# Making the four q units of the sparse attention in the front instead of in the group loop

## The chip, the cores and the metric

The kernel runs on one core of a Trainium2 chip. A core has five engines that run side by side and meet only at semaphores: PE (TensorE, the matrix products; its weight loads are listed apart as PEld), DVE (VectorE), ACT (ScalarE), POOL (GpSimd) and SP (SyncE, which issues DMAs; ACT issues some too). The metric is the device time of one launch in microseconds: the median of several runs.

## The reference, cut to what matters

The program is one transformer block with three mixers, followed by a second block of two layers. The change touches only the first block's input projection and its sparse attention:

```
h = rmsnorm(x, g_pre_mix);  z = h @ w_in                      # x is 512 x 1024
q_nsa, kv_nsa, g_nsa, qkv_ml, if_ml, o_ml, q_mem, g_merge = split(z)
q = q_nsa.reshape(B, S, 4 groups, 4 heads, 64)                # the "q units": 256 columns a group
kc, vc = compress_blocks(k), compress_blocks(v)               # 31 compressed keys and values
o_cmp = masked_softmax(q . kc) @ vc                           # compressed branch
o_slc, o_win = selected and window branches: masked_softmax(q . k) @ v over 512 tokens
y_nsa = gb0 * o_cmp + gb1 * o_slc + gb2 * o_win
h_ml  = mlstm_chunkwise(...)  ->  y_ml = sigmoid(o_ml) * rmsnorm(h_ml) * ml_head_g
y_mem = memory_xattn(...)
gm = sigmoid(g_merge)                                         # three gates of 1024 columns
y = gm0 * (y_nsa @ W_nsa) + gm1 * (y_ml @ W_ml) + gm2 * (y_mem @ W_mem)
```

## The kernel before

**Weights as units.** All weights pass through the same path in units of 1024 x 256 numbers. SP loads a unit into one of two raw buffers; ACT copies it rounded into `w_hi` (L663 in loops, L671 else); POOL subtracts to get the rest, `w_lo` (L1090, L1096; DVE does it in the later feed-forward stages); PE multiplies. Each product is made of three matmuls (hi by hi, hi by lo, lo by hi: L1126 to L1128, or L1154 to L1156 where the result has tokens on the partitions), so one unit is 48 matmuls of 512 columns.

**The front.** The table `UNITS` lists 22 units and `SCHEDULE` writes out by hand in which order units and small steps stand on all engines. The tail of the front is the mLSTM mixer. For each of its four heads, `ml_scores(h)` makes one broadcast product and four score products on PE (L1314, L1319), between which DVE and ACT make the decay and the mask (L1814, L826, L1824, L1827); `ml_out(h)` multiplies by the values (L1330), and then DVE and ACT normalise (L1834 to L1837, L832, L834), which PE waits for before the next head. At the end `ml_norm` scales the result (L1852) and `ml_turn` transposes it on PE (L1340) and splits it on ACT and DVE (L849, L1858).

**The group loop.** The sparse attention runs four times round a loop (one group of four heads each). PE's order in a group: the 48 products of the q unit into banks 0 and 1; 18 matmuls of merge gates (`GATE_PRE`); a wait for `q_split`, while ACT (L875) and DVE (L1884, L1888) split q into the stacked form `q_st`; 16 pairs of compressed scores of 32 columns (L1391, L1392); then 35 steps, each with the scores of step i, the transposes of step i-2 (L1416), the weighting of step i-3 (L1426) and three gate matmuls (L1365); then the transposes of the compressed probabilities (L1442), 12 gate matmuls, the compressed outputs (L1449), the last gate matmuls, and the transposes of the result (L1456). The gate matmuls, 144 in a group, come from three further units and fill PE's time while ACT and DVE work on the softmax. DVE masks the scores (L1930), ACT takes the exponential (L881), both copy the transposed probabilities (L889, L1938). ACT also copies gate tiles out (L899) at the steps named in `GATE_EVAC` and makes `w_hi` of the coming units behind some of these copies. SP loads the eight pieces of the group's keys from DRAM once the group before is finished.

## Time and profile before

| | |
|---|---|
| runs | 3099.30, 3088.74, 3098.14 us; median 3098.14 |
| profiled execution | 3098.84 us, of which 3096.8 us from the first to the last instruction |
| PE busy | 2908.8 us, 94% of the span |
| DVE, ACT, POOL busy | 1467.1, 889.7, 327.5 us |
| mean granted clock of PE | 0.967 of 2.4 GHz |
| mLSTM tail of the front | 273.97 to 371.63 us |
| the four groups | begin at 371.63, 473.36, 573.87 and 672.81 us, merge begins at 774.62 us |

Engines work side by side, so busy times don't add up to the span. A timeline row gives start, length, engine, line, operation, output and inputs, shapes, count, and in brackets the idle time before it and what ended it. PE's single matmuls overlap: how fast they go is the distance of their starts, not their length.

### The profile page before, as it was taken

The page shows a single profiled execution, that of the slowest core. Times are in us where ns is not written, and L with a number is a line of the kernel's source. Part 1 is how long each engine was busy: PE and PEld are TensorE (multiplying, and loading weights), DVE is VectorE, ACT ScalarE, POOL GpSimd, SP SyncE. Part 2 cuts the span into 40 slices and gives each one's busy share as a digit, 9 for nine tenths or more (in the row PEclk, how much of TensorE's full clock was granted, in tenths as well). Part 3 has the DMA queues.
Part 4 walks back from the last instruction along what each step waited for, and adds up shares of the span by engine and source line. Part 5 has one row for each costly group of instructions (what it writes and reads, how often), then busy time and mean ns, then how long its engine had stood idle before and what let it go on. Part 6 is the DMA issues. An engine that isn't in the chain of part 4 may idle for free.

```text
span 3096.8 us, 34841 instructions
## 1 busy us (share of the span) xinstructions
PE 2908.8 (94%) x13510; PEld 2385.9 (77%) x13510; DVE 1467.1 (47%) x2140; ACT 889.7 (29%) x1214; POOL 327.5 (11%) x62
## 2 busy tenths in 40 slices
PE   6998799999998999899999899999999889899997
PEld 6777688888777888778888788887888765578886
DVE  2334344445457443365433644434543479454432
ACT  4333443334233222232222322222222231422221
POOL 4222111111310000000000000000000066100000
PEclk9998899999999999999999999999999999999999
DMA  6222112221441232322232232232223221222221
GB/s 190 87 65 69 55 42 82 72 72 48 142 156 55 95 105 91 102 68 95 95 114 66 81 97 96 98 104 79 95 95 99 78 68 41 68 68 95 96 98 72
DMA packets 255085, 270.54 MB, mean 87 GB/s; under 512 B 5695, under 2 KB 243407, under 8 KB 254858
## 3 DMA queue, kind: packets, MB, share of 16 engines
q1 hardware_dynamic: 250688, 261.87, 26.2%
q10 hardware_dynamic: 4298, 7.36, 0.7%
q8 instruction: 61, 1.00, 0.1%
q14 instruction: 38, 0.31, 0.0%
HBM read 258.72 MB, written 10.49 MB: 87 GB/s over the span
## 4 chain that ended last, share of the span: by engine, by line
PE 71%; issue 16%; POOL 5%; DVE 5%; ACT 2%; DMA 1%; SPq 0%; POOLq 0%; DVEq 0%; ACTq 0%
PE bank L1126 21%; PE bank L1127 20%; PE bank L1128 20%; POOL w_lo L1096 3%; POOL w_lo L1090 3%; PE bank L1620 1%; PE bank L1141 1%; PE bank L1142 1%; PE bank L1143 1%; DVE rstd L2052 1%; ACT w_hi L671 1%; PE bank L1154 1%; PE bank L1156 1%; PE bank L1155 1%; PE bank L1271 0%
## 5 line engine op out<-in xcount | busy, mean ns | idle before, releaser
L1126 PE MATMUL bank<-h_hi,w_hi 128*128 128x512 f32 x2064 | 816.2, 395 | 53.8 <-POOL w_lo L1096 25.4
L1127 PE MATMUL bank<-h_lo,w_hi 128*128 128x512 f32 x2064 | 810.8, 393 | 0.0
L1128 PE MATMUL bank<-h_hi,w_lo 128*128 128x512 f32 x2064 | 810.3, 393 | 0.0
L2008 DVE TENSOR_TENSOR w_lo<-w_raw,w_hi 128x2048 fp32r<-128x2048 f32 (+2 forms) x176 | 390.2, 2219 | 389.1 <-ACT w_hi L671 322.3
L1126 PEld LDWEIGHTS bank<-h_hi,w_hi 128*128 128x128 f32 x2064 | 392.3, 190 | 145.0 <-POOL w_lo L1096 29.6
L1127 PEld LDWEIGHTS bank<-h_lo,w_hi 128*128 128x128 f32 x2064 | 392.3, 190 | 82.6 <-issue 1.2
L1128 PEld LDWEIGHTS bank<-h_hi,w_lo 128*128 128x128 f32 x2064 | 392.0, 190 | 82.3
L1096 POOL TENSOR_TENSOR w_lo<-w_raw,w_hi 128x2048 fp32r<-128x2048 f32 x34 | 217.1, 6391 | 1930.2 <-ACT w_hi L671 1930.2
L1126 PE MATMUL bank<-hid_hi,w_hi 128*128 128x512 f32 x880 | 343.4, 390 | 0.0
L1128 PE MATMUL bank<-hid_hi,w_lo 128*128 128x512 f32 x880 | 342.4, 389 | 0.0
L1127 PE MATMUL bank<-hid_lo,w_hi 128*128 128x512 f32 x880 | 342.4, 389 | 0.0
L663 ACT ACTIVATE w_hi<-w_raw 128x2048 fp32r<-128x2048 f32 x124 | 236.9, 1911 | 355.3 <-PE bank L1128 347.9
L671 ACT ACTIVATE w_hi<-w_raw 128x2048 fp32r<-128x2048 f32 (+2 forms) x110 | 199.5, 1818 | 411.5 <-PE bank L1128 401.5
L964 ACT ACTIVATE gate_tmp<-gate_tmp 128x512 f32<-128x512 f32 x110 | 67.7, 632 | 483.8 <-DVE gate_tmp L2099 483.8
L2107 DVE TENSOR_TENSOR gate_tmp<-gate_tmp,bank 128x512 f32<-128x512 f32 x110 | 75.6, 687 | 252.7 <-PE bank L1128 250.7
L1126 PEld LDWEIGHTS bank<-hid_hi,w_hi 128*128 128x128 f32 x880 | 165.2, 188 | 34.6 <-issue 0.5
L1127 PEld LDWEIGHTS bank<-hid_lo,w_hi 128*128 128x128 f32 x880 | 165.2, 188 | 34.6 <-issue 0.5
L1128 PEld LDWEIGHTS bank<-hid_hi,w_lo 128*128 128x128 f32 x880 | 165.2, 188 | 34.3
L2099 DVE TENSOR_TENSOR gate_tmp<-bank,rstd 128x512 f32<-128x512 f32 x110 | 70.9, 686 | 182.7 <-PE bank L1128 182.5
L1090 POOL TENSOR_TENSOR w_lo<-w_raw,w_hi 128x2048 fp32r<-128x2048 f32 x24 | 110.2, 4594 | 435.3 <-ACT w_hi L663 435.3
L881 ACT ACTIVATE prob<-prob,nsa_stat 128x512 f32<-128x512 f32 (+3 forms) x128 | 71.8, 561 | 158.0 <-DVE nsa_stat L1930 157.9
L1930 DVE CUSTOM_DVE_ANT_0 prob<-bank,const_masks 128x512 f32<-128x512 f32 (+3 forms) x128 | 62.8, 491 | 113.6 <-PE bank L1392 72.5
(362 smaller groups left out, 3437.0 us busy)
## 6 DMA issues: line engine op xcount, KB each, us to landing
w_raw<-in_ffn_w_in_dram SPq DMA_DIRECT2D x88, 1024.0 KB, 5.0
w_raw<-in_w_in_dram SPq DMA_DIRECT2D x32, 1024.0 KB, 5.3
w_raw<-in_ffn_w_out_dram SPq DMA_DIRECT2D x32, 1024.0 KB, 5.0
w_raw<-in_w_ffn_in_dram SPq DMA_DIRECT2D x22, 1024.0 KB, 5.1
w_raw<-in_ffn_w_out_dram SPq DMA_DIRECT2D x16, 768.0 KB, 4.2
w_raw<-in_conv_w_pw_dram SPq DMA_DIRECT2D x12, 1024.0 KB, 5.4
w_raw<-in_w_ffn_down_dram SPq DMA_DIRECT2D x8, 1024.0 KB, 4.9
gate_scratch<-gate_stage ACTq DMA_DIRECT2D x24, 256.0 KB, 2.0
```

What stands on the lines that cost most here:

```text
L663: nc.scalar.activation(w_hi[slot][:, :], raw[s][:, :], ACT.Copy).then_inc(w_hi_ready, 1)
L671: nc.scalar.activation(w_hi[SLOT[u]][:, 0:n], raw[s][:, 0:n], ACT.Copy).then_inc(w_hi_ready, 1)
L881: nc.scalar.activation(prob[i % 4][:, 0:n], prob[i % 4][:, 0:n], ACT.Exp, bias=nmax[:, i:i + 1], scale=-1.0, accum_out=psum_row[:, i:i + 1 ...
L964: nc.scalar.activation(tg[t][:, :], tg[t][:, :], ACT.Silu).then_inc(silu_done, 1)
L1090: nc.gpsimd.tensor_tensor(w_lo[s][:, :], raw[s][:, :], w_hi[s][:, :].bitcast(F32), ALU.subtract).then_inc(w_lo_ready, 1)
L1096: nc.gpsimd.tensor_tensor(w_lo[d][:, :], raw[u % 2][:, :], w_hi[d][:, :].bitcast(F32), ALU.subtract).then_inc(w_lo_ready, 1)
L1126: nc.tensor.matmul(bank[b][:, 0:n], wh, xh, start=first, stop=False)
L1127: nc.tensor.matmul(bank[b][:, 0:n], wh, xl, start=False, stop=False)
L1128: ins = nc.tensor.matmul(bank[b][:, 0:n], wl, xh, start=False, stop=last)
L2008: v.tensor_tensor(w_lo[slot][:, 0:n], raw[s][:, 0:n], w_hi[slot][:, 0:n].bitcast(F32), ALU.subtract).then_inc(w_lo_ready, 1)
L2099: v.tensor_tensor(tg[t][:, :], bank[b + t][:, :], rb[:, :], ALU.mult).then_inc(g_scaled, 1)
L2107: mark(v.tensor_tensor(tg[t][:, :], tg[t][:, :], bank[b + 2 + t][:, :], ALU.mult), up_read, n + (t + 1))
```

## The change

The four q units join the front, one behind each mLSTM head: behind the scores of heads 0 to 2, and behind the output of head 3. ACT and DVE split each into a staging buffer `q_stage`, and ACT issues its store to DRAM (`q_store`, 1 MB each). In the loop SP loads the group's stacked q from there as soon as the group before has transposed its compressed probabilities, and right behind it the eight pieces of keys. A group now opens with the compressed scores, in banks 1 and 5, with one gate matmul behind each of the 16 pairs. DVE splits the compressed keys of the next group at step 9 of the group before. The last gate unit is cut into two half units (1024 x 128), and ACT's weight copies stand at other steps. The diff, cut to its core:

```diff
-         ("in", C_V, UC, "v"), ("in", C_V + UC, UC, "v"), ("in", C_O, UC, "o"), ("in", C_O + UC, UC, "o")]
+         ("in", C_V, UC, "v"), ("in", 0, UC, "q"), ("in", C_V + UC, UC, "v"), ("in", UC, UC, "q"),
+         ("in", C_O, UC, "o"), ("in", 2 * UC, UC, "q"), ("in", C_O + UC, UC, "o"), ("in", 3 * UC, UC, "q")]
...
-             ("ml_scores", 0), ("ml_out", 0), ("unit", 19), ("ml_scores", 1), ("ml_out", 1),
-             ("unit", 20), ("ml_gain", 0), ("ml_norm", 0), ("unit", 21), ("ml_scores", 2), ("ml_out", 2), ("ml_scores", 3),
-             ("ml_gain", 1), ("ml_out", 3), ("ml_norm", 1), ("ml_turn", 0)]
+             ("ml_scores", 0), ("unit", 19), ("ml_out", 0), ("q_store", 0), ("unit", 20), ("ml_scores", 1), ("unit", 21), ("ml_out", 1),
+             ("q_store", 1), ("unit", 22), ("ml_scores", 2), ("unit", 23), ("ml_out", 2), ("q_store", 2), ("ml_gain", 0), ("ml_norm", 0),
+             ("unit", 24), ("ml_scores", 3), ("ml_gain", 1), ("ml_out", 3), ("ml_norm", 1), ("unit", 25), ("q_store", 3), ("ml_turn", 0)]
...
-GATE_PRE, GATE_STEP = 18, 3
-GATE_EVAC = {8: 0, 16: 1, 24: 2, 32: 3}
+GATE_CMP, GATE_STEP = 1, 3
+GATE_EVAC = {6: 0, 13: 1, 21: 2, 29: 3}
...
+GATE_UNIT = (0, 0, 1, 1, 2, 3)
...
+        q_scratch = nc.dram_tensor("q_scratch", [GROUPS, P, HPG * T], F32, kind="Internal").ap()
...
+            sp.wait_ge(q_stored, 16)
+            sp.wait_ge(sT_ready, 4 * TT)
+            sp.sem_inc(c_t, 1)
             with sp.Fori(0, GROUPS) as g:
...
-                load(g * 2 + U_NSA // 2, 0, w_in_t[:, :, bass.ds(g * UC, UC)], KT, UC)
-                gate_load(0)
-                gate_load(1)
-
-
-                sp.wait_ge(y_split, g * 2 + 2)
+                def gate_load(u2, half, c, n):
+                    load(g * 2 + (U_NSA // 2 + u2), half, w_in_t[:, :, bass.ds(g * UC + (C_MERGE + c), n)], KT, n)
+
+                gate_load(0, 0, 0, UC)
+                gate_load(0, 1, D, UC)
+
+                sp.wait_ge(c_t, g + 1)
+                sp.dma_start(q_st[:, :, :].rearrange("p h t -> p (h t)").bitcast(F32),
+                             q_scratch[bass.ds(g, 1), :, :].rearrange("a p n -> p (a n)")).then_inc(q_landed, 16)
+                sp.wait_ge(m_y, 16)
                 for b in range(2):
                     for i in range(2):
                         for half in range(2):
                             sp.dma_start(k_st[b][i][DH * half:DH * (half + 1), :].bitcast(F32),
                                          k_scratch[b, i, bass.ds(g * DH, DH), :]).then_inc(kd_landed, 16)
-                gate_load(2)
+                gate_load(1, 0, 2 * D, P)
+                gate_load(1, 1, 2 * D + P, P)
 
...
+                elif kind == "q":
+                    if TURN_OF[u] > 0:
+                        act.wait_ge(q_stored, 16 * TURN_OF[u])
+                    for h in range(2):
+                        half = slice(DH * h, DH * (h + 1))
+                        ins = nc.scalar.activation(q_stage[half, h, :], b0[half, :], cp)
...
+            def q_store(n):
+                u = UNIT_OF["q"][n]
+                act.wait_ge(evac_act, u + 1)
+                act.wait_ge(evac_dve, DVE_EVACS[u + 1])
+                act.dma_start(q_scratch[n], q_stage[:, :, :].rearrange("p h t -> p (h t)").bitcast(F32)).then_inc(q_stored, 16)
...
-                for h in range(2):
-                    half = slice(DH * h, DH * (h + 1))
-                    nc.scalar.activation(q_st[half, h, :], bank[0][half, :], ACT.Copy).then_inc(q_high, 1)
 
                 def exp_step(i):
                     br, qb, hh = STEPS[i]
...
@@ -909,19 +935,18 @@
                         nc.scalar.activation(p_c[:, :, :, :], p_c[:, :, :, :], ACT.Exp, scale=DH ** -0.5).then_inc(c_e, 1)
                     if i >= 2:
                         turn_step(i - 2)
-                    if i == 2:
-                        high_in_loop(g * 2 + (U_NSA // 2 + 1), 0, 0)
                     if i in GATE_EVAC:
                         gate_evac(GATE_EVAC[i])
                         if GATE_EVAC[i] == 1:
-                            high_in_loop(g * 2 + (U_NSA // 2 + 1), 1, 1)
+                            high_in_loop(g * 2 + (U_NSA // 2 + 1), 0, 0, HALF)
                         if GATE_EVAC[i] == 3:
-                            high_in_loop(g * 2 + (U_NSA // 2 + 2), 0, 0)
-                act.wait_ge(c_t, g + 1)
+                            high_in_loop(g * 2 + (U_NSA // 2 + 1), 1, 1, HALF)
+                act.wait_ge(c_t, g + 2)
                 for qb in range(TT):
                     ins = nc.scalar.activation(pT_c[:, HPG * qb:HPG * (qb + 1), :],
                                                bank[CMP_BANK[qb]][0:NC, :].rearrange("p (h q) -> p h q", q=P), ACT.Copy)
                 ins.then_inc(c_ta, 1)
+                high_in_loop(g * 2 + (U_NSA // 2 + 2), 0, 0)
                 gate_evac(4)
                 gate_evac(5)
 
...
-                    s, out_ = (b + 1) % 2, bank[GATE_BANK[t]][:, :]
+                    b, s = GATE_UNIT[m], GATE_UNIT[m] % 2
+                    out_ = bank[GATE_BANK[m % 2]][:, :]
...
                     if first == 0:
 
                         pe.wait_ge(gt_copied, g * GATE_TILES + (m + 1))
-                        if t == 0:
-                            pe.wait_ge(w_lo_ready, g * 4 + (U_NSA + 2 + b))
+                        if m < 2:
+                            pe.wait_ge(m_lo_s, m + 1)
+                        if m not in (1, 3):
+                            pe.wait_ge(w_lo_ready, g * 4 + (U_NSA + 1 + b))
...
-                pe.wait_ge(w_lo_ready, g * 4 + (U_NSA + 1))
-
-                pe.wait_ge(gt_copied, g * GATE_TILES + 2)
-                products(0, KT, UC, (h_hi, h_lo), (0, 1))
-                gates(GATE_PRE)
-                pe.wait_ge(q_split, g + 1)
-
...
+                pe.wait_ge(q_landed, g * 16 + 16)
+                pe.wait_ge(kc_ready, g + 1)
                 for qb in range(TT):
                     for hh in range(HPG):
                         c = NCP * (2 * qb + hh // 2)
-                        ins = stacked(bank[hh % 2][:, c:c + NCP], hh, qb, [kc_st[0][:, :], kc_st[1][:, :]])
-                ins.then_inc(c_s, 1)
+                        ins = stacked(bank[CMP_S_BANK[hh % 2]][:, c:c + NCP], hh, qb, [kc_st[0][:, :], kc_st[1][:, :]])
+                        if qb == TT - 1 and hh == HPG - 1:
+                            ins.then_inc(c_s, 1)
+                        gates(GATE_CMP)
                 pe.wait_ge(kd_landed, g * 128 + 128)
-
-                pe.wait_ge(y_split, g * 2 + 2)
...
                     if i < NS:
                         scores(i)
+                    if i == 2:
+                        pe.wait_ge(m_lo_s, 4)
+                        pe.wait_ge(y_split, g * 2 + 2)
                     if 2 <= i < NS + 2:
                         turn(i - 2)
                     if i >= 3:
                         weigh(i - 3)
                     gates(GATE_STEP)
...
                     ins = v.tensor_copy(v_sw[u - 10][:, 2:4, :], v1)
                 elif kind == "qk":
-                    ins = v.tensor_copy(qk_in[:, 2 * (u - 14) + 1, 3:3 + T], b1[:, :])
+                    ins = v.tensor_copy(qk_in[:, 2 * TURN_OF[u] + 1, 3:3 + T], b1[:, :])
+                elif kind == "q":
+                    if TURN_OF[u] > 0:
+                        dve.wait_ge(q_stored, 16 * TURN_OF[u])
+                    halves = (slice(0, DH), slice(DH, P))
+                    for h in range(2):
+                        link(v.tensor_scalar(q_stage[halves[h], 2 + h, :], b1[halves[h], :], 1.0, None, ALU.mult))
+                    for h in (2, 3, 0, 1):
+                        if h == 0:
+                            dve.wait_ge(evac_act, u + 1)
+                        own, other = halves[h % 2], halves[1 - h % 2]
+                        ins = v.tensor_tensor(q_stage[other, h, :], bank[2 * (u % 2) + h // 2][own, :],
+                                              q_stage[own, h, :].bitcast(F32), ALU.subtract)
...
+            def compressed_keys(g):
+
+                kc = kcmp[:, bass.ds(g, 1), :].rearrange("p a n -> p (a n)")
+                link(v.tensor_scalar(kc_st[0][:, 0:NC], kc, 1.0, None, ALU.mult))
+                v.tensor_tensor(kc_st[1][:, 0:NC], kc, kc_st[0][:, 0:NC].bitcast(F32), ALU.subtract).then_inc(kc_ready, 1)
+
+            compressed_keys(0)
...
-                dve.wait_ge(w_used, g * 4 + (U_NSA + 1))
-                kc = kcmp[:, bass.ds(g, 1), :].rearrange("p a n -> p (a n)")
-                link(v.tensor_scalar(kc_st[0][:, 0:NC], kc, 1.0, None, ALU.mult))
-                link(v.tensor_tensor(kc_st[1][:, 0:NC], kc, kc_st[0][:, 0:NC].bitcast(F32), ALU.subtract))
-                halves = (slice(0, DH), slice(DH, P))
-                for h in range(2):
-                    link(v.tensor_scalar(q_st[halves[h], 2 + h, :], bank[1][halves[h], :], 1.0, None, ALU.mult))
-                for h in range(HPG):
-                    if h < 2:
-                        dve.wait_ge(q_high, g * 2 + (h + 1))
-                    ins = v.tensor_tensor(q_st[halves[1 - h % 2], h, :], bank[h // 2][halves[h % 2], :],
-                                          q_st[halves[h % 2], h, :].bitcast(F32), ALU.subtract)
-                    if h < HPG - 1:
-                        link(ins)
-                ins.then_inc(q_split, 1)
                 dve.wait_ge(c_s, g + 1)
...
+                between = {1: cmp_max, 2: cmp_shift, 4: cmp_sum, 5: cmp_mask, 6: cmp_gain, 9: lambda: compressed_keys(g + 1)}
```

**PE behind the scores of head 0** (`w_hi_57` and `w_lo_60` are the unit in the odd slot, `v_ml,s_ml` the head's output). Before, and then after:

```order
L1319 MATMUL bank<-qk_in 128x384
L1319 MATMUL bank<-qk_in 128x256
L1319 MATMUL bank<-qk_in 128x128
L1330 MATMUL bank<-v_ml,s_ml 128x129 x10
L1154 MATMUL bank<-w_hi_57,h_hi 128x256
L1155 MATMUL bank<-w_lo_60,h_hi 128x256
L1156 MATMUL bank<-w_hi_57,h_lo 128x256
```

```order
L1344 MATMUL bank<-qk_in 128x384
L1344 MATMUL bank<-qk_in 128x256
L1344 MATMUL bank<-qk_in 128x128
L1151 MATMUL bank<-h_hi,w_hi_57 128x512
L1152 MATMUL bank<-h_lo,w_hi_57 128x512
L1153 MATMUL bank<-h_hi,w_lo_60 128x512
```

The head's output stood directly behind its scores; now the 48 matmuls of a q unit stand between, and the output follows them.

**PE at the opening of a group.** Before, from the last gate matmuls ahead of the compressed scores; then after, from the last product of the fourth q unit to the loop's first rows:

```order
L1365 MATMUL bank<-h_hi,w_hi_57 128x512
L1365 MATMUL bank<-h_lo,w_hi_57 128x512
L1365 MATMUL bank<-h_hi,w_lo_60 128x512
L1386 REGISTER_ALU
L1391 MATMUL bank<-k_cmp_high,q_stacked 128x32
L1392 MATMUL bank<-k_cmp_low,q_stacked 128x32
```

```order
L1153 MATMUL bank<-h_hi,w_lo_60 128x512
L1365 MATMUL bank<-identity_ones,h_ml 128x128 x16
L1376 UNCONDITIONAL_BRANCH
L1376 ISA
L1415 REGISTER_ALU
L1411 MATMUL bank<-k_cmp_high,q_stacked 128x32
L1412 MATMUL bank<-k_cmp_low,q_stacked 128x32
L1384 ISA
L1388 ISA
L1392 MATMUL bank<-h_hi,w_hi_56 128x512
L1411 MATMUL bank<-k_cmp_high,q_stacked 128x32
L1412 MATMUL bank<-k_cmp_low,q_stacked 128x32
```

The q products and the 18 gate matmuls in front of the pairs are gone; one gate matmul stands behind each pair.

**ACT at the end of a group's steps** (`gate_stage` is the copied gate tile, `w_hi` the copy of the coming weights, `pT_cmp` the transposed compressed probabilities). Before, and then after:

```order
L881 ACTIVATE prob_129,nsa_stat<-prob_129,nsa_stat 128x128
L889 ACTIVATE probT_132<-bank 128x128
L896 REGISTER_ALU
L899 ACTIVATE gate_stage_140<-bank 128x512
L900 REGISTER_ALU
L901 ISA
L901 DMA gate_scratch<-gate_stage_140 128x512
L661 ISA
L662 ISA
L663 ACTIVATE w_hi_56<-w_raw_54 128x2048
L922 ACTIVATE pT_cmp<-bank 31x512 x4
```

```order
L907 ACTIVATE prob_128,nsa_stat<-prob_128,nsa_stat 128x128
L922 REGISTER_ALU
L925 ACTIVATE gate_stage_141<-bank 128x512
L926 REGISTER_ALU
L927 ISA
L927 DMA gate_scratch<-gate_stage_141 128x512
L681 ACTIVATE w_hi_57<-w_raw_55 128x1024
L906 REGISTER_ALU
L907 ACTIVATE prob_129,nsa_stat<-prob_129,nsa_stat 128x128
L915 ACTIVATE probT_131<-bank 128x128
L906 REGISTER_ALU
L907 ACTIVATE prob_130,nsa_stat<-prob_130,nsa_stat 128x128
```

The gate copy and a weight copy (now half as wide) stood behind the last exponential; now they stand ahead of the last two, and the full weight copy of the next group's first unit moves behind the four `pT_cmp` copies.

## Rows read from the trace of the kernel before

**Rows 1.** Windows: us, PE, PEld, DVE, ACT, POOL busy, clock, DMA share, GB/s.

```profile
273.97:371.63 97.66, 73.66 (x425) 60.63 (x425) 39.76 (x99) 38.84 (x87) 16.75 (x4) 0.83 0.14 44
...
389.74:402.02 12.28, 11.81 (x57) 10.06 (x58) 4.82 (x13) 3.18 (x8) 0.00 (x0) 0.72 0.00 1
489.65:502.27 12.62, 11.85 (x57) 10.40 (x58) 5.12 (x13) 3.19 (x8) 0.00 (x0) 0.73 0.00 1
590.18:601.09 10.91, 10.21 (x58) 8.72 (x58) 5.05 (x13) 3.19 (x8) 0.00 (x0) 0.84 0.00 1
689.10:699.94 10.84, 10.22 (x58) 8.72 (x58) 4.98 (x13) 3.19 (x8) 0.00 (x0) 0.84 0.00 1
402.02:460.81 58.79, 57.21 (x385) 51.07 (x386) 30.10 (x121) 30.12 (x81) 9.14 (x2) 1.00 0.17 55
...
115.95:127.06 11.11, 11.11 (x50) 9.15 (x49) 2.88 (x8) 3.74 (x9) 4.60 (x1) 1.00 0.00 0
...
262.28:273.97 11.69, 11.69 (x98) 11.56 (x97) 5.91 (x10) 4.66 (x6) 1.67 (x1) 1.00 0.29 92
```

**Rows 2.** Timeline of PE, the mLSTM tail of the front.

```profile
273.97 1.12 PE L1314 MATMUL bank<-gate_row,head_selector 4*128 4x512 f32 x2
...
279.05 0.49 PE L1319 MATMUL bank<-qk_in 128*128 128x128 f32 x2 [0.61 <-DVE s_ml L1827]
...
339.99 2.50 PE L1330 MATMUL bank<-v_ml,s_ml 128*128 128x129 f32 x20 [1.21 <-DVE s_ml L1827]
...
367.90 1.97 PE L1340 MATMUL bank<-identity_ones,h_ml 128*128 128x128 f32 x8 [7.80 <-DVE h_ml L1852]
```

**Rows 3.** DVE's split of the stacked q (min/median/max ns), whole trace.

```profile
L1888 DVE TENSOR_TENSOR q_stacked<-bank,q_stacked x16: 683/688/694, 386.7 to 688.3; 64x512 fp32r<-64x512 f32 x16
```

**Rows 4.** Timeline of DVE and POOL: mLSTM scaling, a convolution step, weight rests.

```profile
324.38 6.57 DVE L1852 SCALAR_TENSOR_TENSOR h_ml<-h_ml,stat,o_ml 128x128 f32<-128x128 f32 x8
...
325.93 4.62 POOL L1096 TENSOR_TENSOR w_lo<-w_raw,w_hi 128x2048 fp32r<-128x2048 f32 x1 [5.65 <-ACT w_hi L671]
...
244.78 4.28 DVE L1744 TENSOR_SCALAR conv_acc<-qk_in,vectors 128x512 f32<-128x512 f32 x1 [0.53 <-ACT qk_in L768]
...
244.29 4.50 POOL L1096 TENSOR_TENSOR w_lo<-w_raw,w_hi 128x2048 fp32r<-128x2048 f32 x1 [11.99 <-ACT w_hi L671]
```

**Rows 5.** Timeline of PE, DVE and ACT at the opening of groups two and three.

```profile
489.65 0.28 PE L1391 MATMUL bank<-k_cmp_high,q_stacked 128*128 128x32 f32 x1 [1.06 <-DVE q_stacked L1888]
489.79 0.26 PE L1392 MATMUL bank<-k_cmp_low,q_stacked 128*128 128x32 f32 x1
489.90 0.26 PE L1391 MATMUL bank<-k_cmp_high,q_stacked 128*128 128x32 f32 x1
...
593.97 0.87 DVE L1895 TENSOR_TENSOR p_cmp<-bank,const_masks 128x248 f32<-128x248 f32 x2 [3.84 <-PE bank L1392]
595.12 0.69 DVE L1930 CUSTOM_DVE_ANT_0 prob<-bank,const_masks 128x512 f32<-128x512 f32 x1 [0.29 <-PE bank L1392]
...
599.50 0.72 ACT L881 ACTIVATE prob<-prob,nsa_stat 128x512 f32<-128x512 f32 x1 [0.74 <-DVE nsa_stat L1930]
...
600.34 0.60 ACT L889 ACTIVATE probT<-bank 128x512 f32<-128x512 f32 x1
```

**Rows 6.** Timeline of PE, then ACT, late in the first group.

```profile
456.89 0.35 PE L1426 MATMUL bank<-v_win,probT 128*128 x2
...
472.51 1.09 PE L1456 MATMUL bank<-identity_ones,y_tok 128*128 128x128 f32 x8 [1.07 <-DVE y_tok L1971]
...
456.42 0.26 ACT L889 ACTIVATE probT<-bank 128x128 f32<-128x128 f32 x1
...
459.61 1.92 ACT L663 ACTIVATE w_hi<-w_raw 128x2048 fp32r<-128x2048 f32 x1 [0.70 <-ACT gate_stage L899]
462.76 2.03 ACT L922 ACTIVATE pT_cmp<-bank 31x512 f32<-31x512 f32 x4 [1.24 <-PE bank L1442]
```

**Rows 7.** DMA issues of the page's last part: size, median us to landing.

```profile
w_raw<-in_w_in_dram SPq DMA_DIRECT2D x32, 1024.0 KB, 5.3
```

89 lines of the change are left out of this document (49 added, 40 removed).

## The prediction

> **What bounds the kernel now.** I read the page first. PE is busy for 94% of the span, and the chain of waits runs mostly on PE, so only PE's idle time and its clock can be won. Then the windows [rows 1]: a q unit's 48 matmuls of 512 columns take 11.11 us at clock 1.00 (115.95 to 127.06, where a unit of the same shape runs), and a token unit 11.69 us. In the middle of a group (402.02 to 460.81) PE is busy 57.21 of 58.79 us at clock 1.00. Two places are worse. The mLSTM tail of the front (273.97 to 371.63) has 97.66 us with PE busy only 73.66, and the clock at 0.83 on average. From the first compressed scores to the first weighting (`v_sel`) each group takes 12.28, 12.62, 10.91 and 10.84 us at clock 0.72 to 0.84. Third, the timeline of PE [rows 2, 5]: in the tail it waits 1.21 us for the mask ahead of a head's output and 7.80 us at the turn; in each group 1.06 us for DVE's last piece of the split q.
>
> The lower clock (1.2 of 2.4 GHz) comes where PE has done little: waits in the tail, and in the openings 16 pairs of matmuls with 32 columns only. There the matmuls stand 0.11 us apart at first (489.79, 489.90), so a pair takes 0.22 [rows 5]; one of 512 columns takes 11.11/48 = 0.23 at full clock [rows 1].
>
> **The change, part by part.**
>
> *Work.* PE's matmuls stay the same in number: 4 x 48 for q move from the groups into the tail of the front, the gate matmuls stay 144 a group. So 4 x 11.11 = 44.4 us change place at no cost, if nothing else waits. New are four stores and four loads of 1 MB, which no compute engine carries.
>
> *The front.* I lay the new order end to end from 273.97. Its scores of a head take 5.57 us (273.97 to 279.54) [rows 2]; heads 1 and 2 the same, 0.4 more at head 2 for ACT's table load. Head 3: 6.0, and 1.5 more, since DVE's eight scaling steps of `ml_norm(0)` now stand directly ahead of it and took 6.57 us in the one case where POOL's 4.62 us ran into them [rows 4]. Heads: 5.6 + 5.6 + 6.0 + 7.5 = 24.7. Outputs: 2.5 us at full clock [rows 2]; three of them now come long after their mask and lose the 1.21 us; the fourth keeps its wait and half the slow clock: 3 x 2.5 + 4.4 = 11.9. Four q units 44.4, three token units 35.1. The turn: 16 transposes, 1.9. Behind it a new wait: DVE first splits the fourth q (six steps of 0.69, 4.4 with gaps [rows 3]), ACT stands in `q_store` behind that and only then copies the four turned tiles, DVE subtracts (four steps of the same length), clears and makes the compressed keys: 9.5 us from the end of the unit, less the 1.9 of the transposes = 7.6. Slow clock: after every head's scores PE has done little, and I charge each following q unit 1.7 us (3.4 us at half speed): 3 x 1.7, as much for the first opening, and half for the fourth q unit: 7.7. Sum: 24.7 + 11.9 + 44.4 + 35.1 + 1.9 + 7.6 + 7.7 = 133.3. Before: 97.66 + 44.4 = 142.1. Gain 8.8 us; bounds: 16 if the clock holds and the last wait halves; 0 if each of the four q splits (4.4) holds up the head behind it by 2 us. In my laying out, a head's h stands ready 5 us before PE asks, so I take 8.8, less 1 for what is rounded: 8.
>
> *The openings.* The 1.06 us wait for the split goes in all four groups [rows 5] (four times, once a group): 4.2. DVE gets the compressed keys a group early, and q comes by DMA. With a gate matmul behind each pair PE has 16 x (0.22 + 0.23) = 7.3 us of work, the same sum as before, half of it in columns of 512, so I expect full clock. From the end of the pairs to the first weighting the chain is then DVE's: two additions 0.87, three masks of 0.69, one maximum about as long, ACT's exponential 0.72 (0.84 to the copy) and copy 0.60 [rows 5], together 5.1, with some eight hand-overs of 0.1 about 6.0. With the pairs' 3.6 that is 9.65 a group against 12.28, 12.62, 10.91, 10.84 = 46.65 [rows 1]: 46.65 - 38.6 = 8.0. Bounds: 4 (the chain slower by 1 us) to 10.
>
> *The end of a group.* Two more gate matmuls stand behind the compressed outputs, where PE waited 1.07 us for DVE's 16 additions (472.51) [rows 6]: 4 x 0.46 = 1.9, which had to be done elsewhere. The full weight copy (1.92) now follows the `pT_cmp` copies (2.03) [rows 6], then POOL (4.6): 8.7 us after the transposes of 462.7, while PE comes to the first gate matmul after 10.9: hidden by 2 us; without this cover it would cost the difference in each group.
>
> *ACT's copies at new steps.* Half of a copy is 0.96. At step 29, ACT now does gate copy, DMA and half copy (the gap of 0.70 after such a copy [rows 6], about as much for the copy itself, and 0.96: 2.2) ahead of the exponential of step 30 and the copy `probT` of step 28, which was at 456.42 with PE taking it at 456.89 [rows 6]. It slips to 458.0, so PE waits 1.2 to 1.3 us: 4 x 1.3 = 5.2 lost. At step 13 the same costs 1.3, but the full copy at step 16 (1.92) goes from among steps of the same kind: 0. Bounds: 0 to 10 together.
>
> *SP.* The q load is queued behind the load of a weight unit, issued about 4 us earlier, and 1 MB lands in 5.3 us [rows 7]. Issued at 462.7 it lands near 468 to 471, PE wants it at 473.4. The pieces of keys follow, wanted 7 us later. Nothing.
>
> Groups: 4.2 + 8.0 + 1.9 - 5.2 - 0.5 (pairs and gates alternating) = 8.4. Total 16.4. From the profiled execution: 3098.84 - 16.4 = 3082.4, rounded to **3082**. That execution stands 0.7 above the median of the runs, which I leave in the range. My own range for this case: 3074 to 3090.
>
> **A rule weighed.** In the trace, a DVE step with two inputs in SBUF (L1852) or one in the fast form (L1744, 4.28 us from 244.78) lasts until POOL's subtraction ends (244.29 + 4.50), while masks and copies from PSUM are untouched [rows 4]. The Trainium skill, page "SBUF — State Buffer", on the shared port pair, says that DVE and GpSimd hold it as an exclusive lock for a whole instruction; the trace agrees. What it would do here is the third rival.
>
> **The rivals.**
>
> *The openings fall to half clock* (slower than before). One gate matmul in three may be too little activity. At half the clock a pair with its gate matmul takes twice the 0.45: 16 x 0.45 = 7.2 a group, and the chain behind loses the 1.3 it had won: 8.5 x 4 less what the waits swallow, 32: 3114. It passes the old time from 4.1 us a group on. Against it: in the steps of 402 to 460.81, too, about half the time goes to gate matmuls and the rest to small ones, and the clock is 1.00 there. Chance 0.06.
>
> *The front gives nothing*: the q splits on DVE and the q stores in ACT's queue stand between a head's output and its normalisation; if the next head waits for it 2 us each and the last wait is 9, 8 us go: 3090. For it: ACT and DVE are in order, and each head's chain gets 4.4 us longer. Against: a whole token unit of 11.69 covers it. Chance 0.14.
>
> *POOL's half units lock DVE*: the half subtraction (2.3 us) behind step 29 runs from about 457.4 to 459.7, over the small two-input step ahead of `y_tok` at 457.9, and the other over the one at step 16. DVE's copy for PE comes 1.5 to 2 us late: 4 x 1.7 = 6.8: 3089. This is what the lock rule says; in the trace no POOL step ran beside these small steps. Chance 0.14.
>
> *More*: the clock does not fall behind the heads (at head 2 it held until the output was done), and the last wait is 5: 3082 - 7 = 3075 or less, down to 3070. Chance 0.16.
>
> *The q load is late*: both loads of 1 MB and the keys share the queues and q lands at 476 instead of by 473.4: 3 x 2.6 = 8: 3090. Chance 0.05.
>
> **How the numbers follow.** My forecast has 0.45, the rivals 0.06, 0.14, 0.14, 0.16, 0.05. A change under 0.5% (15.5 us, about what can be told from none) begins at 3082.6, so my forecast lies on the border: half of its 0.45 is faster by over 0.5%, and the whole of "more", and 0.07 because the runs of before spread over 10 us: 0.46. Slower by over 0.5% (above 3113.6) is half of the first rival and what I don't see: 0.06. The same: 0.48. The range holds all but the half-clock case and the far end of "more": 3070 to 3097.
>
> **What would show it.** Right: PE's wait for the split q (L1391 before) gone and no wait for `q_stacked`'s DMA; windows from the first pair to the first `v_sel` of about 13.3 us with clock near 1.00; 7 to 8 us idle ahead of the first compressed score, ended by DVE; idle time of about 1.3 us at the weighting of step 28, ended by ACT's `probT`. The tail of the front, from the first L1339 row to the first pair, should be 131 to 133 us. Wrong: clock 0.5 in the openings, a gap ended by the DMA of q, POOL's `w_lo` named ahead of the first gate matmul, or a gap between heads ended by ACT's `ml_junk`.

## The result, and the profile after

The changed kernel takes 3082.67 us (median of five runs, 3076.79 to 3084.67), the kernel before 3098.14; the ratio is 0.9948, with a 95% interval of 0.9936 to 0.9960. Run once more as a yardstick it gave 3079.84. The forecast was 3082. Its profiled execution took 3076.79 us against 3098.84: 22.1 less, where 16.4 were forecast. The total came out right while several terms were wrong in opposite directions. One run of a kernel below, the one with the gates ahead, took 7843.86 us; it is in that kernel's median of 3070.50, and the other five have 3069.72.

Windows of the changed kernel, columns as in [rows 1]: the tail of the front with the four q units, then the openings of the four groups (first compressed pair to first `v_sel`), then what is left of groups 1 and 2.

```profile
272.26:399.46 127.20, 108.75 (x617) 90.69 (x617) 60.90 (x126) 53.43 (x101) 34.93 (x8) 0.94 0.32 108
399.46:419.77 20.31, 19.58 (x73) 16.74 (x74) 4.99 (x13) 3.72 (x9) 4.54 (x1) 0.62 0.19 52
494.00:507.17 13.17, 12.44 (x77) 10.53 (x75) 7.64 (x17) 6.28 (x10) 4.57 (x1) 1.00 0.20 60
579.88:592.95 13.07, 12.34 (x77) 10.52 (x75) 7.63 (x17) 6.28 (x11) 4.59 (x1) 1.00 0.23 69
665.62:678.70 13.08, 12.34 (x76) 10.53 (x75) 7.63 (x17) 6.28 (x11) 4.58 (x1) 1.00 0.23 67
419.77:494.00 74.23, 72.05 (x464) 63.96 (x464) 34.72 (x143) 32.09 (x87) 9.26 (x3) 0.95 0.27 82
507.17:579.88 72.71, 70.53 (x463) 62.68 (x464) 34.71 (x143) 32.09 (x87) 9.28 (x3) 0.98 0.26 81
```

The tail was 97.66 us plus 44.4 for the q units; it is 127.20, so 14.9 us went there. PE's idle time in it fell from 24.0 to 18.5 us (window less busy time), which is 5.5. The clock accounts for the other 9: by the mean clock of the two windows (0.83 and 0.94) PE ran some 33 us at half clock before and 15 after. The largest single wait that went is one that the prediction doesn't name. Head 3 stood directly behind head 2 and waited for its normalisation (before):

```profile
346.98 2.07 PE L1314 MATMUL bank<-gate_row,head_selector 4*128 4x512 f32 x2 [4.49 <-ACTq L837]
```

From the first group to the merge it was 402.99 us with the q units, 358.6 without; it is 354.8 (399.46 to 754.27): 3.8 us. Some 1.7 us went ahead of the tail and 1.5 behind the merge's beginning, where nothing was changed; in the kernels below the tail begins at 271.0 to 274.6 us, with no edit ahead of it. Openings 2 to 4 run at full clock where they were at 0.73 to 0.84. The first, at 0.62, takes 7.2 us more than the others.

The timeline of PE around the places of [rows 2], tail of the changed kernel: head 0 and its output, head 3 and its output, the turn (its 16 transposes take 2.93 us together), the first pair.

```profile
277.34 0.49 PE L1344 MATMUL bank<-qk_in 128*128 128x128 f32 x2 [0.61 <-DVE s_ml L1867]
288.57 2.39 PE L1355 MATMUL bank<-v_ml,s_ml 128*128 128x129 f32 x20
...
363.13 1.12 PE L1339 MATMUL bank<-gate_row,head_selector 4*128 4x512 f32 x2
364.18 1.77 PE L1344 MATMUL bank<-qk_in 128*128 128x512 f32 x4
369.52 0.70 PE L1344 MATMUL bank<-qk_in 128*128 128x256 f32 x2 [3.57 <-DVE s_ml L1867]
...
372.53 4.67 PE L1355 MATMUL bank<-v_ml,s_ml 128*128 128x129 f32 x20 [0.90 <-DVE s_ml L1867]
...
390.30 2.08 PE L1365 MATMUL bank<-identity_ones,h_ml 128*128 128x128 f32 x12 [2.03 <-DVE h_ml L1892]
399.46 0.40 PE L1411 MATMUL bank<-k_cmp_high,q_stacked 128*128 128x32 f32 x1 [6.22 <-DVE k_cmp_low L1920]
```

An output behind a unit waits for nothing. The 7.80 us wait at the turn is now 2.03 + 6.22. In the loop the wait for the split q [rows 5] is gone, and no row has PE waiting for q's DMA (issued at 481.21, 5.8 us to landing, wanted at 494.00). In each group PE waits for ACT at the weighting of step 12 and of step 28:

```profile
443.64 0.43 PE L1450 MATMUL bank<-v_sel,probT 128*128 x2 [0.86 <-ACT probT L915]
475.13 0.43 PE L1450 MATMUL bank<-v_win,probT 128*128 x2 [0.72 <-ACT probT L915]
```

### The profile page after: what moved, and what is told of

Its sections match the earlier page's. It is cut to its first block, busy times and chain, and to the rows that moved or that the text cites. A ratio compares the mean times of both kernels' runs of the same rounds, so it can differ in the third digit from the quotient of the medians.

```text
span 3075.0 us, 34891 instructions
## 1 busy us (share of the span) xinstructions
PE 2894.6 (94%) x13510; PEld 2377.6 (77%) x13510; DVE 1472.8 (48%) x2143; ACT 890.0 (29%) x1219; POOL 328.0 (11%) x66
## 4 chain that ended last, share of the span: by engine, by line
PE 72%; issue 15%; DVE 5%; POOL 5%; ACT 2%; DMA 1%; SPq 0%; POOLq 0%; DVEq 0%; ACTq 0%
PE bank L1151 21%; PE bank L1153 21%; PE bank L1152 21%; POOL w_lo L1121 3%; POOL w_lo L1115 2%; PE bank L1648 1%; PE bank L1166 1%; PE bank L1167 1%; PE bank L1168 1%; DVE rstd L2087 1%; PE bank L1179 1%; PE bank L1181 1%; PE bank L1180 1%; ACT w_hi L689 1%; PE bank L1296 0%
## 5 line engine op out<-in xcount | busy, mean ns | idle before, releaser
L1121 POOL TENSOR_TENSOR w_lo<-w_raw,w_hi 128x2048 fp32r<-128x2048 f32 x38 | 235.3, 6196 | 1971.6 <-ACT w_hi L689 1971.6
L681 ACT ACTIVATE w_hi<-w_raw 128x2048 fp32r<-128x2048 f32 (+1 forms) x124 | 230.1, 1855 | 355.2 <-PE bank L1153 347.2
L689 ACT ACTIVATE w_hi<-w_raw 128x2048 fp32r<-128x2048 f32 (+2 forms) x114 | 207.1, 1821 | 412.0 <-PE bank L1153 401.4
L1115 POOL TENSOR_TENSOR w_lo<-w_raw,w_hi 128x2048 fp32r<-128x2048 f32 (+1 forms) x24 | 92.5, 3854 | 371.8 <-ACT w_hi L681 371.8
```

The costliest lines, as they stand in the source:

```text
L681: nc.scalar.activation(w_hi[slot][:, 0:n], raw[s][:, 0:n], ACT.Copy).then_inc(w_hi_ready, 1)
L689: nc.scalar.activation(w_hi[SLOT[u]][:, 0:n], raw[s][:, 0:n], ACT.Copy).then_inc(w_hi_ready, 1)
L1115: nc.gpsimd.tensor_tensor(w_lo[s][:, 0:n], raw[s][:, 0:n], w_hi[s][:, 0:n].bitcast(F32), ALU.subtract).then_inc(w_lo_ready, 1)
L1121: nc.gpsimd.tensor_tensor(w_lo[d][:, :], raw[u % 2][:, :], w_hi[d][:, :].bitcast(F32), ALU.subtract).then_inc(w_lo_ready, 1)
```

## The experiments

Each kernel is the changed one with one edit, unless said otherwise. "Opening" is the window from a group's first pair to its first `v_sel`. In brackets stands the ratio to the kernel before, run on the same chip; the changed kernel's own were 0.9936 to 0.9960, and 0.9929 to 0.9957 when run again.

**The same kernel again.**

> The changed kernel itself, once more, as the yardstick of this set and as a second profiled execution. Theory (the clock's low stretches in the front are drawn anew in each execution): its profile shows one or two stretches of 3.4 us at half clock behind the scores of heads 0 and 2, which the first profile of it lacked, and costs 2 to 5 us more than its 3076.8; median of the runs 3079 to 3083. Rival (the first profile shows the usual course): no low stretch between 250 and 370 us, median 3077.

Measured: 3079.84 us, and a tail of 127.15 us like the first. The median is in the theory's range, but the profile shows no low stretch, as the rival said: the theory fell in this form. But of the kernels below that leave the tail up to the first pair as it is, the one with added matmuls took 127.19, and the pairs first, the later copies, the bare openings and the two loads 130.44, 130.34, 130.41 and 130.41, with 6.8 us more at half clock. Half of it stands behind the scores of head 0 and half behind those of head 2 (of the two loads):

```profile
279.00:282.50 3.50, 3.50 (x10) 2.70 (x9) 0.65 (x3) 1.56 (x1) 1.86 (x1) 0.51 0.44 152
340.50:344.00 3.50, 3.50 (x10) 2.82 (x11) 1.43 (x5) 2.11 (x2) 1.06 (x1) 0.51 0.33 113
```

Of the twelve profiles with the outputs behind the units, seven have these two stretches and five have neither, and both kinds occur on each of the three chips that the experiments ran on. So the same instructions take 127.2 or 130.4 us. No kernel was profiled in both courses, so that it changes from one execution to the next is likely and not shown. The Trainium skill, page "TensorE: Matmul & The Clock Gate", Part 1, calls the number of slow matmuls at a kernel's start run-variable. These rows are from the middle of a kernel; they fit it, and no run here shows it for one kernel.

**Outputs back behind their scores.**

```diff
-("ml_scores", 0), ("unit", 19), ("ml_out", 0),
+("ml_scores", 0), ("ml_out", 0), ("unit", 19),
```

Heads 1 and 2 alike.

> The changed kernel with one part undone: the outputs of heads 0 to 2 stand directly behind their scores again, ahead of the q or token unit that now separates them. Theory (the front's gain over the plain sum comes from this place): three waits of 1.2 us for the mask come back, and the output's 20 small matmuls follow small ones at a clock that falls, 1 to 2 us each: the tail from the first head to the first pair is 6 to 9 us longer, total 3086 to 3089 us against 3080 to 3083. Rival (the waits between heads for h are what the units cover, wherever the output stands): 3.6 us longer at most, 3084 to 3086, with the clock as it is in the changed kernel.

Measured: 3086.92 us (0.9948 to 0.9975), 7.1 more. Windows of the tail, of this kernel and behind it the row of its first output:

```profile
272.53:409.56 137.03, 116.92 (x618) 97.42 (x617) 61.05 (x126) 53.74 (x101) 35.06 (x8) 0.88 0.30 100
```

```profile
279.31 4.67 PE L1355 MATMUL bank<-v_ml,s_ml 128*128 128x129 f32 x20 [1.21 <-DVE s_ml L1867]
```

The tail is 9.9 us longer. Three waits are back (1.21, 1.21, 0.90, together 3.3 us), and each of these outputs takes 4.67 us at half clock where it took 2.39: three times 2.3 is 6.8. The units behind the outputs began slow, some 2 us more, and head 3 gave back as much: it waited 1.42 us instead of 3.57. The theory holds, with more than its 6 to 9 us for the tail: the place of the output is worth more than its waits, because the output itself had been running slow.

**No POOL subtraction beside the scaling of h.**

```diff
-("ml_gain", 0), ("ml_norm", 0), ("unit", 24), ("ml_scores", 3), ("ml_gain", 1), ("ml_out", 3),
+("ml_gain", 0), ("ml_root", 0), ("unit", 24), ("ml_scores", 3), ("ml_norm", 0), ("ml_gain", 1), ("high", 26), ("ml_out", 3),
```

Here `ml_root` is ACT's root, `ml_norm` DVE's scaling, `high` 26 ACT's weight copy.

> The changed kernel with two steps of the front moved so that no POOL subtraction runs beside the scaling of h: DVE's scaling of heads 0 and 1 (8 steps) stands behind the scores of head 3 instead of ahead of them, and ACT's weight copy for the first gate unit (with POOL's subtraction behind it) ahead of the output of head 3. Theory (shared port: a DVE step with two SBUF inputs lasts until POOL's subtraction ends, which is why 8 steps took 6.48 and 6.52 us instead of about 2.2): the wait of 3.57 us in head 3 falls to the 1.4 of the other heads, the wait of 2.03 ahead of the transposes goes, and the last split of q starts at once behind its unit: the first pair comes 4 us earlier, total 3072 to 3073 us against 3076.8. Rival (the eight steps are slow by themselves, or the wait in head 3 comes from ACT's tables, which stand in its queue ahead of the exponentials): the 8 steps still take 6.5 us, and the time does not move by more than 1 us, or gets worse by the 3 us by which the scaling then delays the output of head 3.

Measured: 3077.98 us (0.9923 to 0.9951). DVE's line in the changed kernel, and POOL beside it:

```profile
360.61 6.48 DVE L1892 SCALAR_TENSOR_TENSOR h_ml<-h_ml,stat,o_ml 128x128 f32<-128x128 f32 x8
...
362.15 4.53 POOL L1121 TENSOR_TENSOR w_lo<-w_raw,w_hi 128x2048 fp32r<-128x2048 f32 x1 [16.94 <-ACT w_hi L689]
```

All 16 such steps of this kernel (min/median/max ns), and PE in head 3 and at the turn:

```profile
L1894 DVE SCALAR_TENSOR_TENSOR h_ml<-h_ml,stat,o_ml x16: 344/347/352, 376.3 to 390.3; 128x128 f32<-128x128 f32 x16
```

```profile
373.08 0.70 PE L1346 MATMUL bank<-qk_in 128*128 128x256 f32 x2 [1.56 <-DVE s_ml L1869]
...
390.98 1.91 PE L1367 MATMUL bank<-identity_ones,h_ml 128*128 128x128 f32 x16
400.55 0.39 PE L1413 MATMUL bank<-k_cmp_high,q_stacked 128*128 128x32 f32 x1 [7.66 <-DVE k_cmp_low L1922]
```

No step takes longer than 0.352 us, the waits of 3.57 and 2.03 fall to 1.56 and nothing, and from head 3 to the first pair it is 31.9 us instead of 36.3. The rival fell: the steps are not slow by themselves. The lock of [rows 4] cost up to 4.5 us here. Of these, 2.9 went ahead of the end of the last unit, where the edit also took the eight steps out of the way of head 3's mask; how much of that is the place and how much the lock was not separated. The other 1.6 are behind that unit: from its end to the first pair it is 9.6 us instead of 11.2. The last wait by itself grew from 6.22 to 7.66, since the 2.03 that stood within the same chain is gone. In whole runs the gain is 2 to 5 us and not resolved, and the total is above the 3072 to 3073 us of the theory; this profile's tail has the two low stretches shown above, 3.2 us that the changed kernel's profile lacks.

**Matmuls added in the wait.** Twenty of 512 columns, ahead of the group loop.

```diff
+for _ in range(20):
+    nc.tensor.matmul(bank[5][:, :], h_hi[:, 0, 0:P], h_lo[:, 0, :], start=True, stop=True)
```

> The changed kernel with 20 matmuls of 512 columns added once, ahead of the group loop, in the 6.22 us in which PE waits for the compressed keys; their result is overwritten and used by nothing. Theory (the first opening runs at half clock because PE was idle or small ahead of it, and 7 us are lost by that): the opening of group 1 falls from 20.3 to 13 to 15 us although the program has more work: 5 to 7 us gained, less up to 1 by which the added work outlasts the wait: 3075 to 3077 us against 3080 to 3083. Rival (the pairs with one gate matmul each cannot run at full clock unless a whole group stands ahead, or the first opening is slow for another reason): the opening stays at 20 us, total the same or 1 us more.

Measured: 3080.78 us (0.9929 to 0.9957). The stretch of the added matmuls, the first opening, the second:

```profile
393.00:400.25 7.25, 6.26 (x26) 4.86 (x24) 5.46 (x13) 4.62 (x6) 0.00 (x0) 0.83 0.77 243
400.25:419.57 19.32, 18.77 (x73) 15.93 (x74) 4.90 (x13) 3.64 (x9) 4.55 (x1) 0.65 0.26 67
492.31:505.39 13.08, 12.34 (x77) 10.54 (x75) 7.63 (x17) 6.28 (x11) 4.59 (x1) 1.00 0.23 67
```

The wait fell to 0.99 us and the opening began at full clock, but the clock fell inside it, 2 us behind the first pair, and stayed down for 13.7 us. The theory failed in this form: filling most of the wait does not make the first opening fast. Whether the last 0.99 us of it matters, no run here says.

**The end of the front in another order.** DVE made the compressed keys ahead of the last unit, then subtracted the turned tiles, and split the fourth q last; ACT released the gate banks ahead of its copies of the tiles.

```diff
             def ml_turn(_):
+                act.sem_inc(gt_copied, 2)
...
-("ml_norm", 1), ("unit", 25), ("q_store", 3), ("ml_turn", 0)]
+("ml_norm", 1), ("cmp_keys", 0), ("unit", 25), ("ml_turn", 0), ("q_split", 25), ("q_store", 3)]
```

> The changed kernel with nothing but the end of the front in another order: DVE makes the compressed keys ahead of the last unit, subtracts the turned mLSTM tiles directly behind the transposes and splits the fourth q unit last; ACT stores that q last. The gate matmuls stay one behind each pair. Theory (the 6.22 us wait is this chain, and the half clock of the first opening follows from that wait): the first pair starts within 1 us of the last transpose, 6 us earlier, and the opening runs partly at full clock: 15 to 18 us instead of 20.3, total 8 to 10 us less, 3070 to 3072. Rival (the wait only moves on, and the first opening is slow whatever stands ahead, as with the added matmuls): first pair 5 to 6 us earlier, the opening still about 20 us, a new wait of 1 to 3 us ahead of the first wide scores, which need the split: 3074 to 3078.

Measured: 3066.38 us (0.9888 to 0.9922), 13.5 less than the yardstick. Windows of tail, first and second opening, then PE at the turn:

```profile
271.01:391.57 120.56, 108.43 (x617) 90.72 (x617) 55.22 (x118) 50.44 (x98) 35.15 (x8) 0.96 0.29 98
391.57:405.44 13.87, 13.33 (x76) 11.23 (x74) 10.67 (x19) 6.63 (x11) 3.32 (x1) 0.94 0.54 174
478.05:491.12 13.07, 12.34 (x76) 10.53 (x75) 7.62 (x17) 6.27 (x10) 4.57 (x1) 1.00 0.30 89
```

```profile
389.02 2.90 PE L1365 MATMUL bank<-identity_ones,h_ml 128*128 128x128 f32 x16 [1.97 <-DVE h_ml L1892]
391.57 0.38 PE L1411 MATMUL bank<-k_cmp_high,q_stacked 128*128 128x32 f32 x1
391.79 0.38 PE L1412 MATMUL bank<-k_cmp_low,q_stacked 128*128 128x32 f32 x1
```

No wait is left between the transposes and the first pair: 6.6 us of the tail, and the first opening gives 6.4 more, where the theory had 2 to 5. So the order of three DVE steps behind the last unit held 13 us (ACT's bank release and its store of q moved along with them and were not separated). The slow opening went together with the wait. The clock was at half when the first pair began and came back 1.7 us into the same mix:

```profile
391.57:393.30 1.73, 1.73 (x8) 1.63 (x7) 1.15 (x3) 0.73 (x2) 0.00 (x0) 0.52 0.70 188
393.30:405.44 12.14, 11.60 (x69) 9.60 (x68) 9.53 (x17) 5.90 (x9) 3.32 (x1) 1.00 0.51 172
```

In the changed kernel it stayed at half for 15.5 us of it (399.46 to 415.00). Why 20 wide matmuls in the place of the wait did not keep the clock is open.

**Where the 16 gate matmuls of the opening stand.** Behind the pairs (the first), ahead of them with the turned tiles in banks 1, 5, 6, 7 (the second), or at the group's end with gate copies at steps 8, 16, 24, 32 (the third).

```diff
+                gates(16)
                 pe.wait_ge(q_landed, g * 16 + 16)
...
-                        gates(GATE_CMP)
```

This is the second; the first has the added line behind the loop over the pairs, the third has none.

> The changed kernel with one part undone: in each group the 16 pairs of compressed scores stand together and the 16 gate matmuls behind them. Work and waits are otherwise the same. Theory (the mix holds the clock): in groups 2 to 4, whose openings took 13.17, 13.05 and 13.10 us at clock 1.00, the pairs alone let the clock fall in or behind the opening by one stretch of 3.4 or 6.8 us per group, which costs 1.7 to 3.4 us each, so 5 to 10 us in all, less about 0.9 a group because DVE's two additions then lie beside the gate matmuls: 3079 to 3084 us against 3076.8. Rival (the clock depends on what stands ahead, not on the mix): openings stay at 1.00, DVE's additions are hidden, each opening gets 0.9 us shorter: 3073 us. In group 1, which starts at half clock either way, both say about the same 20 us.

> The changed kernel with the 16 gate matmuls of a group's opening ahead of its 16 pairs instead of one behind each, and the turned mLSTM tiles in banks 1, 5, 6, 7, so that in group 1 the gate matmuls need not wait for them. Theory (the first opening is slow because PE is idle 2.03 and 6.22 us ahead of it and the mix does not bring the clock back): in group 1 the gate matmuls, 3.7 us at full clock, fill more than half of the 6.22 us wait, and the work behind it is shorter by as much: about 4 to 5 us gained in group 1 even if the clock stays down until the first wide scores. In groups 2 to 4 the pairs then stand alone behind 16 wide matmuls: one stretch at half clock each or none, minus 0 to 2 us. Sum: 3 us gained to 3 us lost, 3074 to 3080 us against 3076.8. Rival (the half clock is due to the pairs themselves and the idle time plays no part): group 1 gains nothing beyond what the wait swallows and groups 2 to 4 lose 2 to 3 us each: 3080 us or more.

> The changed kernel with no gate matmul in a group's opening: 16 pairs alone, then the steps, and the 16 gate matmuls behind the transposes of the result at the end of the group; gate copies at steps 8, 16, 24, 32. Theory (the gate matmuls hold the clock): the openings look as before the change, 10.8 to 12.6 us at a clock of 0.70 to 0.84, with a low stretch in each of groups 2 to 4, where the changed kernel has none; the rest of a group is 3.7 us longer, so a group takes 88 us instead of 85.8: 3 x 2.2 lost, but group 1, whose gate matmuls at half clock went with 7.3 us, gains 5: 3080 to 3083 us against 3079.8. Rival (the openings of before were slow for the q unit and its split ahead of them, not for the bare pairs): the clock stays, openings take 9.7, a group 86 us as now, and group 1 gains: 3074 to 3076.

Measured: 3081.43 us (0.9935 to 0.9964), 3070.50 (0.9903 to 0.9935) and 3074.53 (0.9915 to 0.9949). The four openings of the third:

```profile
403.27:417.95 14.68, 14.37 (x57) 12.60 (x58) 4.67 (x11) 3.57 (x8) 4.52 (x1) 0.58 0.28 72
492.51:501.79 9.28, 8.74 (x59) 7.40 (x57) 5.00 (x10) 6.62 (x10) 4.13 (x1) 1.00 0.29 85
575.32:585.76 10.44, 10.10 (x58) 8.65 (x57) 4.99 (x11) 6.72 (x10) 4.59 (x1) 0.84 0.27 75
661.86:673.82 11.96, 11.71 (x59) 9.94 (x57) 4.61 (x11) 6.72 (x10) 4.57 (x1) 0.71 0.28 77
```

Bare pairs lost the clock in two of the groups 2 to 4, pairs ahead of the gates in one (16.23 us at 0.79, then 13.03 twice), gates ahead in one (10.43 at 0.84). With one gate matmul behind each pair, groups 2 to 4 had full clock in all 24 openings of eight profiles. So the mix does hold the clock in the opening, as the theory says, though bare pairs lost it in fewer groups than the theory had. What it doesn't touch is the stretch just ahead. In 21 of these 24 cases PE ran 3.4 to 6.8 us at half clock in the 12 us before the first pair, in the compressed outputs and the wide gate matmuls behind them (changed kernel, groups 1 and 2):

```profile
486.50:493.50 7.00, 7.00 (x23) 5.71 (x23) 3.16 (x16) 0.31 (x1) 2.99 (x1) 0.51 0.83 222
575.20:578.70 3.50, 3.50 (x10) 2.74 (x9) 3.01 (x16) 0.00 (x0) 1.75 (x1) 0.53 0.82 218
```

Before the change the q unit and its gate matmuls stood in these 12 us, at full clock in all three groups, and a low stretch of 3.4 us lay further ahead in two. With bare pairs the low stretch in the opening came twice in place of the one ahead (second kernel, group 2, and third, group 3) and twice on top of it.

And the mix is worth little: the kernel with bare openings is not slower. By the medians it is 5 us faster than the yardstick, by the ratios 3, with intervals that overlap; by the profiles it gained 5.3 us in group 1. Where it had full clock from the first pair on, its opening and the rest of the group take 9.28 + 73.53 = 82.8 us. The changed kernel's group takes 85.8, of which 1.7 are the price of 3.4 us at half clock at its end. That leaves some 1.3 us a group: with the mix PE's 16 gate matmuls hold back the first scores; at the group's end they do not. Its gate copies stand at other steps too, so neither the 1.3 nor the 5 us are the gates' alone.

The first order's rival (0.9 us a group, for DVE's additions) fell: 13.03 against 13.07. In the second kernel it is 7.7 us less from the beginning of the tail to the first pair of group 2, although 16 gate matmuls more stand in that stretch (those of group 2, now ahead of its pairs): group 1's own ran inside the 6.22 us wait. The total is below what theory and rival had.

**ACT's half weight copies two steps later.**

```diff
-                        if GATE_EVAC[i] == 1:
+                    if i == 15:
                             high_in_loop(g * 2 + (U_NSA // 2 + 1), 0, 0, HALF)
-                        if GATE_EVAC[i] == 3:
+                    if i == 31:
                             high_in_loop(g * 2 + (U_NSA // 2 + 1), 1, 1, HALF)
```

> The changed kernel with ACT's two half weight copies of each group two steps later (behind steps 15 and 31 instead of directly behind the gate copies of steps 13 and 29). Theory (the waits of 0.86 us at the weighting of step 12 and of 0.72 us at that of step 28 come from gate copy and half weight copy standing together in ACT's queue): both waits go or fall below 0.3, and a half copy alone (0.98 us) fits between two exponentials, so 4 x 1.2 to 1.5 us are gained: 3071 to 3072 us against 3076.8. Rival (it is the DMA issue and the gate copy alone, the half copy comes when ACT would be idle anyway): both waits stay, and new ones of up to 0.5 us come at the weighting of step 14: 3077 to 3079 us.

Measured: 3078.44 us (0.9927 to 0.9959), no difference that can be told. PE's waits of this kernel that are new:

```profile
454.02 0.43 PE L1450 MATMUL bank<-v_sel,probT 128*128 x2 [0.58 <-DVE probT L1972]
...
483.51 0.50 PE L1392 MATMUL bank<-h_hi,w_hi 128*128 128x512 f32 x1 [0.42 <-POOL w_lo L1115]
```

The waits of 0.86 and 0.72 went, so they did come from gate copy and weight copy together; but 1.0 of the 1.58 us came back. The gain of 1.2 to 1.5 a group was wrong, though the cause was right.

**Two loads of q**, the keys behind both.

```diff
+                sp.wait_ge(q_landed, g * 32 + 16)
+                sp.dma_start(q_st[:, :, :].rearrange("p h t -> p (h t)").bitcast(F32),
+                             q_scratch[bass.ds(g, 1), :, :].rearrange("a p n -> p (a n)")).then_inc(q_landed, 16)
...
-                pe.wait_ge(q_landed, g * 16 + 16)
+                pe.wait_ge(q_landed, g * 32 + 32)
```

> The changed kernel with the load of q made twice in every group, the second behind the landing of the first, and the keys behind both. Theory (the load is hidden, with 7 us of cover: issued at 481.21, 5.8 us to landing, wanted at 494.0): the second lands at about 493, a wait of 0 to 1 us at the first pair and none at the first scores, whose keys then land about 498 and are wanted at 501.4: total the same, 0 to 4 us more than 3079.8. Rival (the cover is thin, 2 to 5 us as forecast, or the queues are shared with the weights and each load then takes longer): 3 to 5 us of waiting in each group, 9 to 15 us more, 3089 to 3095.

Measured: 3084.79 us (0.9941 to 0.9975). PE's row at the first pair of group 2 has no wait:

```profile
497.23 1.08 PE L1487 MATMUL bank<-identity_ones,y_tok 128*128 128x128 f32 x7
498.07 0.26 PE L1414 MATMUL bank<-k_cmp_high,q_stacked 128*128 128x32 f32 x1
```

Its groups take 94.66, 85.77 and 85.74 us against 94.54, 85.88 and 85.74. The load is hidden, with room for another. The profile accounts for 3.2 us of the extra time by the tail (130.41); the rest of the median isn't explained.

**What they point to, together.** Gates ahead, no lock and the new end of the front; the pairs then wait for two turned tiles. The diff is that between this kernel and the same with half the gate matmuls among the pairs.

```diff
-                gates(16)
+                gates(8)
...
+                        if hh % 2 == 0:
+                            gates(1)
```

> What the runs so far point to, together: the 16 gate matmuls ahead of the pairs (group 1 fills its wait with them), no POOL subtraction beside the scaling of h, and at the end of the front DVE makes the compressed keys first, then splits the turned mLSTM tiles, and last the fourth q unit, so that the first pair waits for two tiles alone. Theory (the waits of 3.57, 2.03 and 6.22 us and the half clock of the first opening are one chain behind the last unit, each separately removable): the first pair comes about 5 us behind the transposes, no wait over 1 us between the last unit and the first pair, clock full in the opening; 7 to 10 us less than with the gate matmuls ahead alone (3070.5): 3061 to 3064 us. Rival (the gains overlap: gate matmuls already fill the wait, and a shorter chain only moves the wait to the first scores, which need the split of the fourth q unit): 2 to 4 us less than 3070.5: 3067 to 3069 us.

> The kernel with both improvements (gate matmuls ahead, no lock, short chain at the end of the front), with 8 of the 16 gate matmuls ahead of the pairs and one behind every second pair. Theory (the openings of that kernel lost the clock for 3.4 to 6.8 us because bare pairs follow, and the mix would hold it): low stretches in the openings of groups 1 to 3 go, 3 to 5 us gained against its 3066.4, so 3062 to 3064. Rival (the clock there is a matter of where the stretches happen to fall, and gate matmuls between the pairs push back the start of DVE's chain by 1.8 us a group): 3067 to 3070.

Measured: 3066.38 us (0.9887 to 0.9922) and 3063.26 (0.9875 to 0.9914). The openings of groups 1 to 3, first without the mix, then with:

```profile
393.89:404.94 11.05, 10.34 (x58) 8.57 (x57) 8.53 (x16) 5.90 (x9) 3.27 (x1) 0.85 0.54 177
483.69:495.73 12.04, 11.71 (x59) 10.04 (x57) 4.68 (x11) 3.22 (x8) 4.52 (x1) 0.72 0.17 44
571.40:582.09 10.69, 10.11 (x59) 8.65 (x57) 4.93 (x13) 3.02 (x8) 4.26 (x1) 0.84 0.19 49
```

```profile
391.29:403.84 12.55, 10.68 (x66) 9.13 (x66) 11.41 (x18) 5.80 (x9) 2.83 (x1) 1.00 0.53 173
481.19:492.31 11.12, 10.58 (x66) 8.90 (x65) 5.67 (x15) 4.94 (x10) 4.57 (x1) 1.00 0.18 47
566.89:578.04 11.15, 10.62 (x67) 8.91 (x65) 5.71 (x15) 5.18 (x10) 4.58 (x1) 1.00 0.18 47
```

The first has a tail 6.1 us shorter than with the gates ahead alone (121.93 against 127.98), but its openings lost the clock and gave 3.7 of it back (33.8 us for groups 1 to 3 against 30.1): the total moved 3 to 4 us, what the rival said, and not the theory's 7 to 10. With the mix all four openings are at 1.00. 3063.26 us is 1.1% less than before and the best of all kernels here; over the new end of the front alone (3066.38) it is 3 us, within the intervals.

## Why the prediction was right, point by point

- *Work moved at no cost*: right. The q units took 11.0 us each (the last 11.4), and the bare sum of 44.4 held.
- *Front*: 133.3 forecast, 127.2 measured. The term that failed is "slow clock 7.7": the clock stayed full through the first three q units and up to head 3 (277.58 to 370.40). What was charged did come in the other course of the same tail (130.4), behind heads 0 and 2 and not behind head 1. The prediction has no row for its 3.4 us a piece; the stretches measured there are that long. Heads and outputs, forecast 36.6, took 36.6; the lock in head 3 was there, and larger (3.57 us of waiting instead of 1.42 + 1.5). Not foreseen: the same lock holds the last scaling (6.52 us), hence the 2.03 us ahead of the turn, whose transposes took 2.93 us instead of 1.9, partly at half clock. The last wait, forecast 7.6, was 6.22.
- *Openings*: 13.3 us forecast, 13.17, 13.07 and 13.08 measured, at full clock; but 20.31 in group 1. So of 8.0 us, 1.6 came. The rival of half clock came true where a wait stood ahead, in one group of four, though the wait alone doesn't explain it (the added matmuls); it should have had its price there, 7 us, with a chance of its own. Split wait: 4.2 us, right.
- *ACT's copies*: 1.3 us forecast at step 28, nothing at step 13; measured 0.72 and 0.86. With the smaller waits around, a group had 1.35 us of such waits before (0.38, 0.27, 0.70) and 2.17 after: 3.3 us lost in four groups instead of 5.2.
- *End of the group, SP*: the 1.07 us wait for DVE's additions is gone, right; q's load is hidden, with 7 us of cover where 2.4 to 5.4 were reckoned, right.
- *POOL's half units lock DVE*: they do. One small step of DVE, beside POOL's half subtraction at 474.54 (2.37 us, to 476.91), takes 1.70 us, to 476.93, where the 32 steps of its kind have a median of 0.165. A copy from PSUM beside the same subtraction takes 0.29, so what the prediction says of masks and copies from PSUM, which [rows 4] don't show, is so here:

```profile
L1978 DVE TENSOR_TENSOR nsa_stat<-nsa_stat,nsa_gate x32: 162/165/1709, 431.8 to 737.8; 128x4 f32<-128x4 f32 x32
...
474.71 0.29 DVE L1972 COPY probT<-bank 128x128 f32<-128x128 f32 x1
...
475.23 1.70 DVE L1978 TENSOR_TENSOR nsa_stat<-nsa_stat,nsa_gate 128x4 f32<-128x4 f32 x1
```

But no wait of PE follows from it: price 0, not 6.8. The rule of the Trainium skill that the prediction weighed ("SBUF — State Buffer", shared port pair) holds in both places; where it cost time was the front, beside whole units.

So the groups gave 3.8 us instead of 8.4, the front 14.9 instead of 8, and 3 us lay where nothing was changed. Most of the mechanism was right: work moved at no cost, outputs without their waits, the openings of groups 2 to 4, the split wait, the hidden load. The match of the total is in part luck: the front gave 6.9 us more than forecast and the openings 6.4 less.

## What to carry to other kernels

Put long matmul work between a short dependent chain's link and the next, so that small matmuls neither wait nor run slow; the place of the output was worth three times its waits (9.9 us against 3.3). Then look at what stands directly behind the last piece of work before a loop: there the order of three DVE steps cost 13 us, more than half of the 22 that the whole change brought by the profiles. And price a wait together with what runs behind it: the 6 us wait and 6 to 7 us of slow work behind it went together, though filling the wait with other work did not remove the slow part.

## What the runs showed of the hardware

- Sixteen pairs of 32-column matmuls by themselves lost the full clock in two of three groups; with one matmul of 512 columns behind each pair they kept it in all 24 openings of groups 2 to 4 of the eight kernels that have this mix (13.07 to 13.17 us each).
- Once at half clock, the same mix stayed there for 15.5 us in the changed kernel, behind a wait of 6.22 us; with no wait ahead, in the new end of the front, the clock was back 1.7 us into it.
- Twenty wide matmuls ahead of it (full clock from 395.5) did not keep the clock beyond 402.2 us, with 0.99 us of waiting between them and the first pair. No run here says why.
- A DVE step of 4 columns with two SBUF inputs lasted until the end of the POOL subtraction that it met (1.70 us, one case), as the long ones do.
- The same tail takes 127.2 or 130.4 us by where half clock falls, in kernels whose instructions are the same up to there.
